# Making the next group's weights behind the up product instead of between the two products of a step

## The chip, the cores and the metric

The kernel runs on one core of one Trainium2 chip. The metric is the device time of one execution in microseconds. The engines are named as in the profile: PE is the matmul engine (PEld its weight loads), DVE the vector engine, ACT the activation engine, POOL and SP the two that mostly issue DMAs.

## What is computed

The reference is one inference step of a trunk layer with attention, retention and, last, an expert retrieval (PEER). Only the last part matters here. For every token, 128 of 16384 single-neuron experts are picked (8 heads, 16 each), and

```python
act = jax.nn.gelu(jnp.einsum('thkd,td->thk', u_table[eidx], xb), approximate=False)
return jnp.einsum('thk,thkd->td', g * act, v_table[eidx])
```

There are 1152 tokens, 1024 features, and tables `u_table` and `v_table` of 16384 x 1024.

## The kernel before

The stage that the change touches, `stage_experts`, treats the tokens in two ways. The first 384 tokens (three tiles of 128, "sparse") gather their experts' rows by indirect DMA (L2019); DVE multiplies them (L2107 in the first half, L2120 in the second). The other 768 tokens ("dense") go through all 16384 experts, in two groups of 384 tokens. A group takes J = 128 steps. Step n loads 128 experts' columns of u and v and does:

- the **down product** (`down`, L2193 to L2202): `p_a` = u times h, 24 matmuls of 384 columns, in three parts: u_hi with h_hi, u_hi with h_lo, u_lo with h_hi. `p_a` is one PSUM bank and not doubled, so the product waits until the GELU of the step before has read it (`gelu_full`). It also waits for `u_hi` (ACT, L1976) and, before its last 8 matmuls, for `u_lo` (DVE, L2082).
- the GELU (ACT, L1986), which reads `p_a`, and DVE's product of it with the experts' weights of these tokens (L2095), split into `g_hi` (L2098) and `g_lo` (L2100).
- the **up product** (`up`, L2204 to L2233): `p_y` += g times v, 18 matmuls of 512 columns, which need `g_hi`, `v_lo` and `g_lo`.

The weights of a group are a dense table that has to be made first: WeightSteps makes it in 96 steps of 4 tokens. DVE makes one-hot tiles `hot_j`, `hot_i` and `hot_w` (L1791 to L1795), PE multiplies them with 8 matmuls of 128 columns into the bank `pw` (`tensor`, L1804), and ACT copies `pw` out to `wt` (`scalar`, L1812, called the **copy** below). The first group's weights are made ahead of the loop. The second group's are made inside the first group's loop, one weight step in each of its first 96 turns. There is one bank `pw` there (`one_bank`).

`blocks` (L1885) writes the loop of every engine. One turn j calls `pre` for step j + 2 and `post` for step j + 1. On PE `pre` is the down product and `post` the up product, and the weight step of turn j stands between them. On ACT, whose `late` is set, a turn is `u_hi` of step j + 2, the GELU of step j + 1, `v_hi` of step j + 2 and then the copy of weight step j:

```python
                pre(j + (o + 2), j + 2, s)
                if weighted and not late:
                    weights(j + w.STEPS, s)
                post(j + (o + 1), j + 1, 1 - s)
```

On DVE a turn is `u_lo` of step j + 2, the one-hot tiles of weight step j, the three small products of step j + 1, the sparse products of one rank, and `v_lo` of step j + 2. Every engine runs its queue in the order written; engines are tied to each other by semaphores alone. The copy waits for `pw_full`, which PE's last matmul of the weight step raises.

Of the kernel before, what the change touches and what calls it, by code (L numbers as in the profile page):

```python
# [1080 lines left out]
def wait_count(eng, sem, count):  # L1081

    if not isinstance(count, int) or count > 0:
        eng.wait_ge(sem, count)
# [737 lines left out]
def stage_experts(nc, sem, m, keep, a):  # L1822
# [16 lines left out]
    w = WeightSteps(nc, sem, m, keep, keep.pairsT[:, 2, DENSE_AT:DENSE_AT + N_KEYS * WeightSteps.IN // 2].bitcast(F16))  # L1839
# [13 lines left out]
    one_bank = [pw[:]]  # L1853
# [24 lines left out]
    def weight_steps(eng, body):  # L1878
        body(0, 0)
        body(1, 1)  # L1880
        with eng.Fori(1, w.STEPS // 2) as k:
            for s in range(2):
                body(k * 2 + s, s)

    def blocks(eng, g, pre, post, first=lambda: None, between=lambda: None, weights=lambda n, s: None, late=None, rest=lambda n: None, unroll=False):  # L1885

        both = lambda n, j, s: (pre(n, j, s), late(n, j, s) if late else None)  # L1890
        o = g * J
        both(o, 0, 0)
        both(o + 1, 1, 1)
        first()
        post(o, 0, 0)
        between()

        def turn(k, weighted):
            for s in range(2):
                j = k * 2 + s  # L1900
                pre(j + (o + 2), j + 2, s)
                if weighted and not late:
                    weights(j + w.STEPS, s)
                post(j + (o + 1), j + 1, 1 - s)
                if late:
                    late(j + (o + 2), j + 2, s)
                if weighted and late:
                    weights(j + w.STEPS, s)
                rest(j)

        def turns(lo, hi, weighted):
            if unroll:
                for k in range(lo, hi):
                    turn(k, weighted)
            else:
                with eng.Fori(lo, hi) as k:
                    turn(k, weighted)

        done = w.STEPS // 2 if g < GROUPS - 1 else 0
        if done:  # L1920
            turns(0, done, True)
        turns(done, J // 2 - 1, False)
        post(o + J - 1, J - 1, 1)
# [5 lines left out]
    with nc.Block() as block:  # L1929

        @block.sync
        def _(sp):
            for s in range(SPARSE):
                sp.dma_start(hs[s], keep.h2_dram[:, :, s * P:(s + 1) * P]).then_inc(cols_in[s], 16)

            def load(n, j, s):
                wait_count(sp, ulo_full, n - 1)
                sp.dma_start(u_raw[s][:], a["uT"][j]).then_inc(u_in[s], 16)
                wait_count(sp, vlo_full, n - 1)
                sp.dma_start(v_raw[s][:], a["v"][j]).then_inc(v_in[s], 16)  # L1940

            for g in range(GROUPS):
                def first():
                    if g == 0:
                        w.store(sp, 0, w.stored)
                        with sp.Fori(1, BLOCKS) as b:
                            w.store(sp, b, w.stored)

                blocks(sp, g, load, lambda n, j, s: None, first)
            sp.wait_ge(ulo_full, GROUPS * J)  # L1950
            sp.wait_ge(vlo_full, GROUPS * J)
            for s in range(SPARSE):
                sp.dma_start(x1_sparse[s], keep.x1_dram[s]).then_inc(xs_in, 16)
            for s in range(SPARSE):
                sp.wait_ge(sparse_full, s + 1)
                sp.dma_start(out_rows(s), x1_sparse[s]).then_inc(sparse_out, 16)
            for i in range(GROUP):
                sp.wait_ge(y_full, (GROUPS - 1) * GROUP + i + 1)
                sp.dma_start(out_rows(SPARSE + (GROUPS - 1) * GROUP + i), x1[i][:]).then_inc(y_out[1][i], 16)
            sp.wait_ge(sparse_out, 16 * SPARSE)  # L1960
            for g in range(GROUPS):
                for i in range(GROUP):
                    sp.wait_ge(y_out[g][i], 16)
# [209 lines left out]
        @block.tensor  # L2173
        def _(pe):
            pe.sem_inc(w.pw_full, w.LEAD)
            pe.sem_inc(y_step, 1)
            for r in range(3):
                for s in range(SPARSE):
                    last = nc.tensor.transpose(p_idx[r][:, s * P:(s + 1) * P], keep.pairsT[:, r, s * P:(s + 1) * P], keep.ident)
            last.then_inc(idx_full, 1)  # L2180
            for s in range(SPARSE):
                pe.wait_ge(cols_in[s], 16)
                wait_count(pe, cols_read, s)
                for k in range(KD):
                    last = nc.tensor.transpose(p_h[:, k * P:(k + 1) * P], hs[s][:, k, :], keep.ident)
                last.then_inc(cols_turned, 1)
            weight_steps(pe, lambda n, s: w.tensor(pe, n, s, two_banks))
            pe.wait_ge(idx_done, 2)
            pe.wait_ge(cols_read, SPARSE)
            pe.wait_ge(w.pw_read, w.STEPS + w.LEAD)  # L2190

            for g in range(GROUPS):
                def down(n, j, s):  # L2193
                    pe.wait_ge(uhi_full, n + 1)
                    wait_count(pe, gelu_full, n)
                    for k in range(KD):
                        nc.tensor.matmul(p_a[:, 0:GT], u_hi[s][:, k, :], h_hi[:, k, :], start=k == 0, stop=False)  # L2197
                        nc.tensor.matmul(p_a[:, 0:GT], u_hi[s][:, k, :], h_lo[:, k, :], start=False, stop=False)  # L2198
                    pe.wait_ge(ulo_full, n + 1)
                    for k in range(KD):  # L2200
                        last = nc.tensor.matmul(p_a[:, 0:GT], u_lo[s][:, k, :], h_hi[:, k, :], start=False, stop=k == KD - 1)  # L2201
                    last.then_inc(a_full, 1)  # L2202

                def up(n, j, s):  # L2204
                    pe.wait_ge(ghi_full, n + 1)
                    pe.wait_ge(vlo_full, n + 1)
                    first, end = (isinstance(j, int) and j == x for x in (0, J - 1))
                    if first:
                        wait_count(pe, y_mul, g * GROUP)

                    def product(i, part, vv, begin, stop):
                        for half in range(2):
                            last = nc.tensor.matmul(p_y[i][:, half, :], part[s][:, i * P:(i + 1) * P], vv[s][:, half * 512:(half + 1) * 512],  # L2213
                                                    start=begin, stop=stop)
                        return last

                    if end:
                        pe.wait_ge(glo_full, n + 1)
                        for i in range(GROUP):
                            product(i, g_hi, v_hi, False, False)  # L2220
                            product(i, g_hi, v_lo, False, False)
                            last = product(i, g_lo, v_hi, False, True)
                            last.then_inc(y_tile, 1)
                        pe.wait_ge(y_tile, (g + 1) * GROUP)
                        pe.sem_inc(y_step, 1)
                        return
                    for i in range(GROUP):
                        product(i, g_hi, v_hi, first, False)
                        product(i, g_hi, v_lo, False, False)
                    pe.wait_ge(glo_full, n + 1)  # L2230
                    for i in range(GROUP):
                        last = product(i, g_lo, v_hi, False, False)
                    last.then_inc(y_step, 1)  # L2233

                pe.wait_ge(h_lo_full, g + 1)
                blocks(pe, g, down, up, weights=lambda n, s: w.tensor(pe, n, s, one_bank))

# [120 lines left out]
```

## Time and profile before

| | us |
|---|---|
| median of 3 runs | 4092.27 (4087.77 to 4099.85) |
| the profiled execution | 4092.37 |
| its span (first to last instruction) | 4090.6 |
| outside the span | 1.8 |

The execution is profiled once. In the views a row of the timeline is: start in us, duration in us, engine, line and operation, out<-in, and in brackets the idle time of that engine before it with what ended it. Matmuls are pipelined: a record's duration contains a tail that overlaps the next matmul, so the pace of PE is read from starts and not from durations. The first group's loop with weight steps runs from about 1882 to 2755 us, the second group's loop from about 2800 to 4050 us.

### The profile page before, as it was taken

How to read it: one execution, taken by the hardware profiler on the slowest of the kernel's cores; microseconds unless marked ns; L12 is line 12 of the kernel's file. 1: busy time of each engine (PE TensorE's matmuls, PEld its weight loads, DVE VectorE, ACT ScalarE, POOL GpSimd, SP SyncE). 2: the span in 40 equal slices, each digit the busy share in tenths (PEclk: the TensorE clock that was granted, in tenths of full speed). 3: DMA queues.
4: the chain of work that ended last, by engine and by line, in shares of the span. 5: the costliest groups of instructions: out<-in, count | busy, mean ns of one | idle time of the engine just before them, and what ended most of it. 6: DMA issues, size and time to landing. Idle time of an engine off the chain costs nothing.

```text
span 4090.6 us, 58626 instructions
## 1 busy us (share of the span) xinstructions
PE 3728.8 (91%) x19218; PEld 3036.7 (74%) x19218; DVE 2990.6 (73%) x5999; ACT 1231.1 (30%) x1750; POOL 1675.8 (41%) x1065
## 2 busy tenths in 40 slices
PE   8799988997669997278999999999999999999998
PEld 1699964665554443157888888888988999999997
DVE  0322273333534999798999999998889888888888
ACT  0411052222222222273333333332332233223222
POOL 0222100000311232204555555555557677777764
PEclk9799987998789999558999999999999999999999
DMA  7288713665241010348999999999999999999997
GB/s 255 100 267 288 253 38 103 205 201 188 80 150 52 31 36 21 113 185 289 331 339 343 349 340 342 343 339 363 341 307 370 361 340 340 344 335 344 331 347 256
DMA packets 302338, 1018.08 MB, mean 249 GB/s; under 512 B 30410, under 2 KB 61932, under 8 KB 294948
## 3 DMA queue, kind: packets, MB, share of 16 engines
q1 hardware_dynamic: 153348, 483.34, 35.1%
q0 software_dynamic: 128880, 486.07, 32.5%
q10 hardware_dynamic: 20016, 47.66, 3.0%
q8 instruction: 30, 0.49, 0.1%
q14 instruction: 64, 0.52, 0.0%
HBM read 875.22 MB, written 141.72 MB: 249 GB/s over the span
## 4 chain that ended last, share of the span: by engine, by line
PE 31%; DVE 14%; DMA 6%; issue 6%; POOL 1%; ACT 0%; DVEq 0%; ACTq 0%; SPq 0%; POOLq 0%
PE p_y L2213 16%; DVE rows L2107 6%; PE p_a L2201 5%; PE p_a L2198 5%; PE p_a L2197 5%; DMA rows<-u_rows,pairsT 5%; DVE u_lo L2082 2%; DVE v_lo L2089 2%; DVE hot_w L1795 1%; POOL rows L2019 1%; DVE pairsT L2095 1%; DVE g_hi L2098 1%; DMA rows<-in_v,pairsT 1%; DVE hot_j L1791 1%; DMA w_ring<-weights_spill 0%
## 5 line engine op out<-in xcount | busy, mean ns | idle before, releaser
L2019 POOL DMA_INDIRECT rows<-in_v,pairsT x384 | 730.2, 1902 | 300.5 <-DVE h_rows L2120 207.5
L2019 POOL DMA_INDIRECT rows<-u_rows,pairsT x384 | 594.8, 1549 | 492.2 <-DVE pairsT L2107 419.8
L2197 PE MATMUL p_a<-h_hi,u_hi 128*128 128x384 f32 x2048 | 687.5, 336 | 4.1 <-DVE h_lo L2160 2.4
L2198 PE MATMUL p_a<-h_lo,u_hi 128*128 128x384 f32 x2048 | 691.0, 337 | 0.0
L1981 ACT ACTIVATE v_hi<-v_raw 128x1024 fp32r<-128x1024 f32 x256 | 272.0, 1063 | 750.1 <-PE p_y L2213 735.5
L2213 PE MATMUL p_y<-v_hi,g_hi 128*128 128x512 f32 x1536 | 489.7, 400 | 7.9 <-DVE g_hi L2098 7.5
L2107 DVE CUSTOM_DVE_ANT_0 rows<-rows,h_rows 128x1024 f32<-128x1024 f32 x384 | 451.6, 1221 | 53.8 <-DMA rows<-u_rows,pairsT 51.1
L2120 DVE SCALAR_TENSOR_TENSOR h_rows<-rows,pairsT,h_rows 128x1024 f32<-128x1024 f32 x381 | 467.8, 1280 | 18.9 <-DMA rows<-in_v,pairsT 18.9
L2213 PE MATMUL p_y<-v_lo,g_hi 128*128 128x512 f32 x1536 | 478.6, 393 | 0.0
L2201 PE MATMUL p_a<-h_hi,u_lo 128*128 128x384 f32 x2048 | 400.1, 336 | 20.6 <-DVE u_lo L2082 20.6
L2197 PEld LDWEIGHTS p_a<-h_hi,u_hi 128*128 128x128 f32 x2048 | 385.3, 188 | 15.1 <-issue 4.6
L2198 PEld LDWEIGHTS p_a<-h_lo,u_hi 128*128 128x128 f32 x2048 | 385.1, 188 | 9.8
L2213 PE MATMUL p_y<-v_hi,g_lo 128*128 128x512 f32 x1536 | 390.6, 389 | 0.0
L2201 PEld LDWEIGHTS p_a<-h_hi,u_lo 128*128 128x128 f32 x2048 | 359.3, 188 | 25.1 <-DVE u_lo L2082 25.1
L2213 PEld LDWEIGHTS p_y<-v_lo,g_hi 128*128 128x128 f32 x1536 | 289.9, 189 | 66.4
L2213 PEld LDWEIGHTS p_y<-v_hi,g_lo 128*128 128x128 f32 x1536 | 288.7, 188 | 60.0
L2213 PEld LDWEIGHTS p_y<-v_hi,g_hi 128*128 128x128 f32 x1536 | 280.2, 189 | 54.6 <-DVE g_hi L2098 10.2
L2082 DVE TENSOR_TENSOR u_lo<-u_raw,u_hi 128x1024 fp32r<-128x1024 f32 x256 | 311.9, 1219 | 6.0 <-ACT u_hi L1976 6.0
L2089 DVE TENSOR_TENSOR v_lo<-v_raw,v_hi 128x1024 fp32r<-128x1024 f32 x256 | 312.4, 1221 | 1.3 <-issue 1.0
L1812 ACT ACTIVATE wt<-pw 128x512 f32 (+1 forms) x144 | 156.3, 1085 | 409.8 <-PE pw L1804 399.1
L1976 ACT ACTIVATE u_hi<-u_raw 128x1024 fp32r<-128x1024 f32 x256 | 270.0, 1055 | 4.8 <-DMA u_raw<-in_uT 4.8
L1522 PE MATMUL psc<-wc,hs 128*128 128x512 f32 x576 | 251.5, 595 | 0.0
(308 smaller groups left out, 5625.9 us busy)
## 6 DMA issues: line engine op xcount, KB each, us to landing
u_raw<-in_uT SPq DMA_DIRECT2D x256, 512.0 KB
v_raw<-in_v SPq DMA_DIRECT2D x256, 512.0 KB
w_ring<-weights_spill POOLq DMA_DIRECT2D x32, 1536.0 KB
u_rows<-pairsT ACTq DMA_DIRECT2D x64, 512.0 KB
key_cols<-in_uT SPq DMA_DIRECT2D x64, 512.0 KB, 4.1
u_rows<-key_rows SPq DMA_DIRECT2D x64, 512.0 KB
wada<-in_w_ada SPq DMA_DIRECT2D x12, 2048.0 KB, 8.0
weights_spill<-wt SPq DMA_DIRECT2D x24, 1024.0 KB, 3.9
```

What stands on the lines that cost most here:

```text
L1522: last = nc.tensor.matmul(psc[:, 4 * b:4 * b + 4, :], hs[:, k, :], wc[:, k, 4 * b:4 * b + 4, :], start=k == 0, stop=k == KD - 1)
L1976: nc.scalar.activation(u_hi[s][:], u_raw[s][:], ACT.Copy).then_inc(uhi_full, 1)
L1981: nc.scalar.activation(v_hi[s][:], v_raw[s][:], ACT.Copy).then_inc(vhi_full, 1)
L2019: pool.indirect_dma_start(rows[s][n % SLOTS][:], None, (keep.u_rows, v_rows)[g], at).then_inc(rows_in[s][n % SLOTS], 16)
L2082: nc.vector.tensor_sub(u_lo[s][:], u_raw[s][:], u_hi[s][:].bitcast(F32)).then_inc(ulo_full, 1)
L2089: nc.vector.tensor_sub(v_lo[s][:], v_raw[s][:], v_hi[s][:].bitcast(F32)).then_inc(vlo_full, 1)
L2107: nc.vector.tensor_tensor_reduce(out=slot[:], in0=slot[:], in1=keep.h_rows[:, s, :], op0=ALU.mult, op1=ALU.add, scale=1.0, scalar=0.0, acc ...
L2120: nc.vector.scalar_tensor_tensor(out=total, in0=slot[:], scalar=share, in1=total, op0=ALU.mult, op1=ALU.add).then_inc(rows_used, 1)
L2197: nc.tensor.matmul(p_a[:, 0:GT], u_hi[s][:, k, :], h_hi[:, k, :], start=k == 0, stop=False)
L2198: nc.tensor.matmul(p_a[:, 0:GT], u_hi[s][:, k, :], h_lo[:, k, :], start=False, stop=False)
L2201: last = nc.tensor.matmul(p_a[:, 0:GT], u_lo[s][:, k, :], h_hi[:, k, :], start=False, stop=k == KD - 1)
L2213: last = nc.tensor.matmul(p_y[i][:, half, :], part[s][:, i * P:(i + 1) * P], vv[s][:, half * 512:(half + 1) * 512], start=begin, stop=stop)
```

## The change

`blocks` gets a parameter `after`. PE alone passes `after=True`, and with it the weight step of a turn stands behind `post` (the up product) instead of between `pre` and `post`. The other engines' code is the same.

```diff
-    def blocks(eng, g, pre, post, first=lambda: None, between=lambda: None, weights=lambda n, s: None, late=None, rest=lambda n: None, unroll=False):
+    def blocks(eng, g, pre, post, first=lambda: None, between=lambda: None, weights=lambda n, s: None, late=None, rest=lambda n: None, unroll=False, after=False):
...
                 pre(j + (o + 2), j + 2, s)
-                if weighted and not late:
+                if weighted and not late and not after:
                     weights(j + w.STEPS, s)
                 post(j + (o + 1), j + 1, 1 - s)
+                if weighted and after:
+                    weights(j + w.STEPS, s)
                 if late:
                     late(j + (o + 2), j + 2, s)
...
-                blocks(pe, g, down, up, weights=lambda n, s: w.tensor(pe, n, s, one_bank))
+                blocks(pe, g, down, up, weights=lambda n, s: w.tensor(pe, n, s, one_bank), after=True)
```

The first place on PE is the seam between the down and the up product of a turn in the first group's loop. Lines behind L1902 are numbered two higher in the changed kernel. `p_a<-h_hi,u_lo` is the end of the down product, `pw` the weight step, `p_y` the up product. Before:

```order
L2201 MATMUL p_a<-h_hi,u_lo 128x384 x8
L1800 REGISTER_ALU
L1801 REGISTER_ALU
L1804 MATMUL pw<-hot_w,hot_i 128x128 x8
L2213 MATMUL p_y<-v_hi,g_hi 128x512 x2
```

In the changed kernel:

```order
L2200 MATMUL p_a<-h_lo,u_hi 128x384
L2203 MATMUL p_a<-h_hi,u_lo 128x384 x8
L2215 MATMUL p_y<-v_hi,g_hi 128x512 x2
L2215 MATMUL p_y<-v_lo,g_hi 128x512 x2
L2215 MATMUL p_y<-v_hi,g_hi 128x512 x2
```

The eight matmuls into `pw` and the two register instructions ahead of them have left this place.

The second place on PE is the seam between the up product of one turn and the down product of the next. Before:

```order
L2213 MATMUL p_y<-v_lo,g_hi 128x512 x2
L2213 MATMUL p_y<-v_hi,g_lo 128x512 x6
L2194 REGISTER_ALU
L2197 MATMUL p_a<-h_hi,u_hi 128x384
L2198 MATMUL p_a<-h_lo,u_hi 128x384
```

In the changed kernel:

```order
L2215 MATMUL p_y<-v_hi,g_lo 128x512 x6
L1800 REGISTER_ALU
L1801 REGISTER_ALU
L1804 MATMUL pw<-hot_w,hot_i 128x128 x8
L2196 REGISTER_ALU
L2199 MATMUL p_a<-h_hi,u_hi 128x384
L2200 MATMUL p_a<-h_lo,u_hi 128x384
```

The weight step is now the last thing ahead of the next down product.

ACT's queue keeps its order. This is one turn's copy (`wt<-pw`) and what follows it in the changed kernel (`pairsT<-p_a` is the GELU):

```order
L1812 ACTIVATE wt<-pw 128x4x128
L1978 ACTIVATE u_hi<-u_raw 128x1024
L1986 REGISTER_ALU
L1988 ACTIVATE pairsT<-p_a 128x384
L1983 ACTIVATE v_hi<-v_raw 128x1024
```

Nothing moved here: `u_hi` of the next turn and the GELU stand behind the copy, before and now.

## Rows read from the trace of the kernel before

**Rows 1.** The page: granted clock in 40 slices; the chain by engine

```profile
PEclk9799987998789999558999999999999999999999
...
PE 31%; DVE 14%; DMA 6%; issue 6%; POOL 1%; ACT 0%; DVEq 0%; ACTq 0%; SPq 0%; POOLq 0%
```

**Rows 2.** Busy time by stretch: window, length, engines, clock, DMA share, GB/s

```profile
2000.00:2700.00 700.00, 693.11 (x3901) 619.46 (x3900) 660.54 (x1167) 264.72 (x312) 389.58 (x263) 1.00 0.95 342
3000.00:4000.00 1000.00, 996.11 (x5034) 905.87 (x5033) 893.34 (x970) 301.51 (x361) 709.15 (x381) 1.00 0.96 343
```

**Rows 3.** Waits from 1880 to 2750 us: total us, times, longest us

```profile
ACT wt L1812 <- PE pw L1804: 379.4, 94, 10.6
...
PE p_a L2201 <- DVE u_lo L2082: 15.0, 10, 4.8
```

**Rows 4.** Timeline of one turn, first group's loop with weight steps

```profile
2007.78 0.64 PE L1804 MATMUL pw<-hot_w,hot_i 128*128 128x128 f16 x8
...
2008.23 0.71 PE L2213 MATMUL p_y<-v_hi,g_hi 128*128 128x512 f32 x2
...
2008.77 1.11 ACT L1812 ACTIVATE wt<-pw 128x512 f32 x1 [3.86 <-PE pw L1804]
...
2009.67 1.08 ACT L1976 ACTIVATE u_hi<-u_raw 128x1024 fp32r<-128x1024 f32 x1
...
2010.63 0.48 ACT L1986 ACTIVATE pairsT<-p_a 128x384 f32<-128x384 f32 x1
2010.78 1.23 DVE L2082 TENSOR_TENSOR u_lo<-u_raw,u_hi 128x1024 fp32r<-128x1024 f32 x1 [0.25 <-ACT u_hi L1976]
...
2012.20 0.19 PEld L2197 LDWEIGHTS p_a<-h_hi,u_hi 128*128 128x128 f32 x1
...
2013.85 0.36 DVE L2098 CAST g_hi<-pairsT 128x384 fp32r<-128x384 f32 x1
...
2015.22 1.55 PE L2201 MATMUL p_a<-h_hi,u_lo 128*128 128x384 f32 x8
...
2016.62 0.64 PE L1804 MATMUL pw<-hot_w,hot_i 128*128 128x128 f16 x8
...
2017.06 0.70 PE L2213 MATMUL p_y<-v_hi,g_hi 128*128 128x512 f32 x2
...
2017.60 1.10 ACT L1812 ACTIVATE wt<-pw 128x512 f32 x1 [3.85 <-PE pw L1804]
```

**Rows 5.** Timeline of PE alone: five idle times between 2.6 and 3.2 us

```profile
2780.14 2.16 PE L2201 MATMUL p_a<-h_hi,u_lo 128*128 128x384 f32 x8 [2.68 <-DVE u_lo L2082]
...
1963.31 1.66 PE L2201 MATMUL p_a<-h_hi,u_lo 128*128 128x384 f32 x8 [2.69 <-DVE u_lo L2082]
...
1588.05 1.09 PE L1516 MATMUL pT<-grid,xn 128*128 128x128 f32 x8 [2.71 <-ACT xn L1587]
...
1192.27 1.91 PE L1548 MATMUL psc<-sc 128*128 128x128 f32 x15 [2.83 <-ACT wc L1619]
...
1039.03 0.63 PE L1207 MATMUL bank_qf<-grid,qf 128*128 128x128 f32 x4 [3.17 <-issue]
```

**Rows 6.** Busy time in short stretches behind these idle times, columns as Rows 2

```profile
2778.00:2782.00 4.00, 1.86 (x8) 1.86 (x9) 3.93 (x6) 0.00 (x0) 2.60 (x2) 0.89 0.88 284
2782.00:2786.00 4.00, 4.00 (x14) 3.24 (x14) 4.00 (x7) 0.49 (x1) 2.61 (x2) 0.69 0.96 370
...
1963.00:1967.00 4.00, 3.50 (x22) 2.95 (x23) 3.11 (x8) 1.21 (x2) 2.10 (x2) 1.00 1.02 329
...
1589.00:1593.00 4.00, 0.49 (x4) 0.38 (x3) 4.00 (x4) 3.55 (x9) 2.27 (x1) 0.61 0.00 0
...
1193.00:1197.00 4.00, 3.15 (x28) 2.96 (x26) 1.38 (x2) 1.19 (x2) 0.00 (x0) 1.00 0.41 136
...
1039.00:1043.00 4.00, 3.97 (x25) 4.00 (x25) 1.38 (x2) 1.88 (x2) 2.42 (x2) 0.66 0.00 0
```

**Rows 7.** Busy time while the first group's weights are made, columns as Rows 2

```profile
1750.00:1800.00 50.00, 36.82 (x286) 27.32 (x284) 49.44 (x144) 37.63 (x37) 0.00 (x0) 0.50 0.46 189
```

## The prediction

> **What bounds the kernel now.** I read the page's slices first, then busy time by stretch, then the waits of the stretch that the change touches, then the timeline of one turn. The clock line shows where the two dense groups run: the last twenty slices or so, almost all at full clock [rows 1]. By stretch, PE is busy for 693 of 700 us in the first group's loop and 996 of 1000 us in the second, where no weights are made [rows 2]. Both are at granted clock 1.00, that is 2.4 GHz. DVE follows at 661 of 700 us. The chain of waits names PE most [rows 1]. So in the first group's loop PE sets the pace and DVE has little to spare. ACT is busy for 265 of 700 us, and the waits say what it does with the rest: for 379 us, in 94 waits, it stood in front of the copy of `pw` until PE had made it [rows 3].
>
> The timeline of a turn shows the pace: the weight step starts at 2007.78 and again at 2016.62, so a turn lasts 8.84 us [rows 4]. Within it PE does the weight step (2007.78 to 2008.23, 0.45 us), the up product until about 2012.4, and the down product until the next weight step. The reader should see one thing more. ACT's copy starts at 2008.77, 0.99 us behind the start of the weight step; `u_hi` of the next turn starts at 2009.67, the GELU at 2010.63, and it ends at 2011.11. ACT had been idle for 3.86 us before the copy, though `u_raw` and `p_a` were there earlier: these two stand behind the copy in its queue and are held up by it. PE needs both of their results for the next down product, whose first weight load starts at 2012.20. They were ready 1.09 us before that. The up product, some 4 us of PE's own work, is what hides the copy, `u_hi` and the GELU.
>
> **What the change removes and adds.** No instruction comes or goes. PE still does 8 matmuls into `pw` in each of 96 turns, 0.45 us of its time, and the two register instructions move along. Removed is the weight step from the seam between down and up product: the up product can start 0.45 us earlier behind the down product. This is worth nothing by itself, since PE is full. Nor does it uncover a wait: `g_hi` starts at 2013.85 and takes 0.36 us, so it is there at 2014.21, and the up product starts at 2017.06 [rows 4], 2.85 us later; 0.45 us less leaves 2.4.
>
> Added is a closed chain at the other seam. PE's weight step ends the turn; ACT's copy waits for it; `u_hi` and the GELU stand behind the copy; and PE's next down product waits for both. The up product that used to cover this now stands ahead of it. Nothing else lies between, so PE stands still. Step by step from the start of the weight step [rows 4]: 0.99 us to the start of the copy, 0.90 to the start of `u_hi`, 0.96 to the start of the GELU, 0.48 for the GELU: 3.33 us. PE has worked 0.45 of this. Its restart is not seen in these rows; the starts behind other waits bound it between 0 and some 0.3 us (the weight load of 0.19 us at 2012.20 and a hand-over), and I take 0.17. The stall is 3.33 - 0.45 + 0.17 = 3.05 us in each turn, between 2.9 and 3.2. In the profile it will read about 0.2 less, since a record of matmuls has a tail (0.64 us for the weight step, against 0.45 to the next start [rows 4]).
>
> Who else waits? DVE's `u_lo` waits for `u_hi` (0.25 us now [rows 4]) and comes later by the same amount; the down product needs `u_lo` only for its last 8 matmuls, some 2.8 us behind its start, and `u_lo`, which starts with the GELU and takes 1.23 us against its 0.48, ends some 0.7 us behind the start. DVE is behind `u_lo` as it was, and a turn of nearly 12 us is longer than its 8.4 us of work (661 us in 79 turns [rows 2]), so it will be idle instead of late. `v_hi` stands behind the GELU and is not needed before the up product of a later step. POOL's and SP's queues are tied to DVE's and PE's progress and get slack. The next turn's one-hot tiles are made long before PE asks for them, and the bank `pw` is free, since the copy is in the chain anyway. So the chain closes on PE alone: 8.84 + 3.05 = 11.89 us for a turn at full clock, and 96 x 3.05 = 293 us in all.
>
> **The clock.** A stall of this size in every turn can also lower PE's clock. The trace has five idle times of PE between 2.6 and 3.2 us [rows 5]. Behind the one of 2.68 us the clock was 0.89 and 0.69 in the two next stretches of 4 us [rows 6]: at the lower of the two levels, 1.2 GHz, that is 2 x (0.11 + 0.31) x 4 = 3.4 us. Behind the one of 2.69 us it stayed at 1.00, behind 2.71 it fell (0.61), behind 2.83 it stayed, behind 3.17 it fell (0.66) [rows 5, 6]. So three of five fell, and length alone did not decide. My stall reads as 2.85 us, in the upper part of these. A fall costs half of the low stretch, since PE has nothing but work then: 1.7 us. Per turn the price lies between 0 and 1.7 us. I take nine falls in ten, 1.5 us, nearer the upper end: the stall is longer than four of the five, and where three of five idle times single out at random fall, a stall in every turn meets any condition that depends on when it comes.
>
> The Trainium skill, "TensorE: Matmul & The Clock Gate", section "HAM oscillation — how this bites in real kernels", says that a loop in which PE waits between bursts of matmuls can start every pass at the lower clock. By that rule the price is the full 1.7 us, and the sum below would be 4540 us; the two idle times without a fall (2.69 and 2.83 us [rows 5, 6]) do not follow it.
>
> **The sum.** 8.84 + 3.05 + 1.5 = 13.4 us for a turn. 96 x 4.55 = 437 us. Against this, PE's present waits for `u_lo` in this loop, 15.0 us in 10 waits [rows 3], come from gathers that are late for DVE; with several us to spare in each turn about half of them should vanish: -8 us. Against the profiled execution's 4092.4 us, which is the median of the runs within 0.1 us, this gives 4092 + 437 - 8 = 4521 us.
>
> **Rivals.**
>
> *The clock stays up.* Then only the stall is paid: 4092 + 293 - 8 = 4377 us, or 4363 to 4391 for stalls of 2.9 to 3.2 us. For it speak the idle times of 2.69 and 2.83 us; against it the other three, and that there are 96 stalls to come.
>
> *The clock stays down for longer.* If a low stretch lasts twice as long (it was 3.4 us in the clean case, but PE at half speed meets its next stall sooner), the price is 3.4 us: 96 x 6.45 - 8 = 611, so 4703 us. While the first group's weights are made, the clock stood at 0.50 throughout with PE busy for 36.8 of 50 us [rows 7]. Those are short bursts, with a pause about every 1.4 us; here PE works for over 8 us without a break, so this is the lesser case.
>
> *The other side: the copy is not what holds ACT up.* If ACT could take `u_hi` and the GELU ahead of the copy, or if PE's down product did not have to wait for the GELU, the chain would be open. The up product would start 0.45 us earlier, PE would remain full, and the time would be 4092 us, or some 15 us less if the 0.16 us of pause in front of the weight step vanished with its move (96 x 0.16). It decides from where the GELU would end less than 0.45 us behind the weight step's start. The queue's order and the single bank `p_a` speak against it: the GELU started at 2010.63, 2.85 us behind the start of the weight step, and its input stands ahead of that step on PE, so it waited for nothing but the queue.
>
> *The change does less than it says*, because some turns are not reached by it: the new order stands in the one loop body that runs all 96 turns, so there is little room.
>
> **How the numbers follow.** The forecast, a closed chain with a fall of the clock in most turns: 0.70. Clock stays up: 0.13. Clock down for longer: 0.11. Something between the forecast and the second: 0.03. Not slower: 0.03. The forecast's own bounds are 96 x (2.9 + 1.0) to 96 x (3.2 + 1.8), which is 4459 to 4564 us. The range is to leave out no more than 2 in 10: it takes in the case with full clock, 4363, and ends at 4600, a little above the forecast's own upper bound, since that bound knows the low stretch from one clean case; it leaves out most of the last two cases. A measurement of this kernel can tell 0.3% from no change, some 12 us. Faster by over 0.3%: 0.01. Within 0.3%: 0.02. Slower: 0.97.
>
> **What would show it.** The waits should have a row that isn't there now, PE's first down matmul waiting for ACT's GELU, about 96 times for 2.85 us, some 275 us in total. The starts of the weight steps should be 13.4 us apart, or 11.9 where the clock is up. The distances on ACT from copy to `u_hi` to GELU should be the same 0.9 and 0.96 us. The granted clock in this loop should be near 0.88 (low for about 3.1 of 13.4 us), DVE's share should fall from 94% to some 62%, and the second group's loop should be as before. The forecast is wrong if PE's wait is for something else, if it is under 2.5 us, or if the clock is 1.00 throughout.

## The result

The changed kernel took 4467.01 us (median of 4 runs, 4464.08 to 4469.12) against 4090.02 us for the kernel before in the same comparison (4083.7 to 4099.85). The ratio of the times is 1.0919, with a 95% interval of 1.0895 to 1.0942. It is slower by 377 us; 4521 us was predicted, with a range of 4363 to 4600.

The page of the changed kernel, sections 2 and 4 (the chain of waits by engine, then by line), answers to [rows 1]:

```profile
PEclk9899889996899975688888889889999999999999
...
PE 50%; issue 5%; ACT 3%; DVE 1%; ACTq 1%; DMA 1%; POOL 0%; SPq 0%; DVEq 0%; POOLq 0%
PE p_y L2215 23%; PE p_a L2199 9%; PE p_a L2200 9%; PE p_a L2203 8%; ACT u_hi L1978 2%; PE pw L1804 1%; ACT pairsT L1988 1%; DMA rows<-in_v,pairsT 1%; ACTq L1812 1%; DVE h_rows L2122 0%; POOL rows L2021 0%; DMA w_ring<-weights_spill 0%; ACTq L1809 0%; ACTq L1918 0%; DVE u_lo L2084 0%
```

Two things are new. In the first group's loop the clock line now has eights, where the kernel before has nines, and ACT is in the chain: its lines for `u_hi` and for the GELU (`pairsT`), and L1812 on ACT's own sequencer (ACTq), which is register work for the copy.

Busy time by stretch in the changed kernel (window, length, PE, PEld, DVE, ACT, POOL, clock, DMA share, GB/s), for the two groups' loops, answers to [rows 2]:

```profile
2000.00:3100.00 1100.00, 873.18 (x4236) 780.77 (x4235) 722.54 (x1270) 268.62 (x336) 411.26 (x286) 0.89 0.71 237
3400.00:4400.00 1000.00, 997.49 (x5035) 907.65 (x5034) 890.21 (x969) 299.79 (x360) 728.57 (x386) 1.00 0.96 343
```

The second group's loop is what it was: 5035 matmuls in 1000 us against 5034. In the first group's loop PE is busy for 79% where it was 99%, DVE for 66% where it was 94%, and the clock is 0.89.

The matmuls of the weight steps in this loop, by line, in the kernel before (first row) and in the changed one (second row), with the starts of the first and the last matmul:

```profile
L1804 PE MATMUL pw<-hot_w,hot_i x768: 218/218/330, 1881.9 to 2745.4; 128*128 128x128 f16 x192
```

```profile
L1804 PE MATMUL pw<-hot_w,hot_i x768: 218/218/234, 1889.8 to 3125.4; 128*128 128x128 f16 x192
```

They are 96 steps of 8. The mean turn was 863.5 / 95 = 9.09 us and is 1235.6 / 95 = 13.01 us. (The last matmul starts 0.4 us behind the start of its step; this adds under 0.005 us to either mean.) That is 372 us in 95 turns, of 376.7 us by which the spans differ (4467.3 against 4090.6). So the loss lies in this loop.

The waits of the changed kernel from 1880 to 3130 us (who waited for whom: us in total, times, longest us) answer to [rows 3]:

```profile
ACT wt L1812 <- PE pw L1804: 939.3, 96, 10.2
...
DVE u_lo L2084 <- ACT u_hi L1978: 419.1, 96, 8.0
PE p_a L2199 <- ACT pairsT L1988: 259.3, 96, 2.8
```

The row that the prediction asked for is there: PE's first down matmul waits for ACT's GELU, 96 times, 2.70 us each. PE's wait for `u_lo` [rows 3] is gone from this stretch.

The timeline of one seam in the changed kernel answers to [rows 4]:

```profile
2410.74 0.64 PE L1804 MATMUL pw<-hot_w,hot_i 128*128 128x128 f16 x8
2411.72 1.02 ACT L1812 ACTIVATE wt<-pw 128x512 f32 x1 [10.06 <-PE pw L1804]
2412.55 1.05 ACT L1978 ACTIVATE u_hi<-u_raw 128x1024 fp32r<-128x1024 f32 x1
2413.49 0.48 ACT L1988 ACTIVATE pairsT<-p_a 128x384 f32<-128x384 f32 x1
...
2414.12 0.41 PE L2199 MATMUL p_a<-h_hi,u_hi 128*128 128x384 f32 x1 [2.75 <-ACT pairsT L1988]
```

Read from top to bottom it is the closed chain: weight step, copy 0.98 us later, `u_hi` 0.83 us later, GELU 0.94 us later, 0.48 us for it, and PE 0.15 us behind its end. From the weight step's start to the next down product are 3.38 us; the weight step's own work is 0.45 of them.

The starts of three weight steps in a row in the timeline of PE alone, with the restarts between them, show two kinds of turns:

```profile
2372.43 0.64 PE L1804 MATMUL pw<-hot_w,hot_i 128*128 128x128 f16 x8
2375.72 0.45 PE L2199 MATMUL p_a<-h_hi,u_hi 128*128 128x384 f32 x1 [2.66 <-ACT pairsT L1988]
2384.14 0.64 PE L1804 MATMUL pw<-hot_w,hot_i 128*128 128x128 f16 x8
2387.53 0.46 PE L2199 MATMUL p_a<-h_hi,u_hi 128*128 128x384 f32 x1 [2.74 <-ACT pairsT L1988]
2397.48 0.64 PE L1804 MATMUL pw<-hot_w,hot_i 128*128 128x128 f16 x8
```

From 2372.43 to 2384.14 are 11.71 us, from 2384.14 to 2397.48 are 13.34. Over the 95 distances 18 are short (mean 11.72) and 77 long (mean 13.30). The idle time is 2.69 us on the mean of the short ones and 2.70 on that of the long ones; what differs is how long PE's work behind it takes. (The restarts come 3.29 and 3.39 us behind the weight step in turn, here as in the whole loop, so the mean is 3.34.) Busy time in stretches of 4 us in the changed kernel, columns as before, shows why:

```profile
2398.00:2402.00 4.00, 1.35 (x7) 1.24 (x6) 1.63 (x3) 3.20 (x4) 2.06 (x2) 0.93 0.99 375
2402.00:2406.00 4.00, 4.00 (x17) 4.00 (x17) 3.93 (x9) 0.00 (x0) 0.19 (x1) 0.65 0.97 322
2406.00:2410.00 4.00, 4.00 (x20) 3.41 (x19) 2.97 (x5) 0.00 (x0) 3.51 (x2) 1.00 0.97 296
```

Behind the idle time that ends at 2400.77 the clock stood at its lower level of 1.2 GHz for 2 x (0.07 + 0.35) x 4 = 3.4 us, with PE busy all the while.

### The profile page after: what moved, and what is told of

It is laid out like the page before. It is cut to its first block, busy times and chain, and to the rows that moved or that the text cites. A ratio compares the mean times of both kernels' runs of the same rounds, so it can differ in the third digit from the quotient of the medians.

```text
span 4467.3 us, 58626 instructions
## 1 busy us (share of the span) xinstructions
PE 3866.1 (87%) x19218; PEld 3162.8 (71%) x19218; DVE 2989.5 (67%) x5999; ACT 1211.8 (27%) x1750; POOL 1667.8 (37%) x1065
## 4 chain that ended last, share of the span: by engine, by line
PE 50%; issue 5%; ACT 3%; DVE 1%; ACTq 1%; DMA 1%; POOL 0%; SPq 0%; DVEq 0%; POOLq 0%
PE p_y L2215 23%; PE p_a L2199 9%; PE p_a L2200 9%; PE p_a L2203 8%; ACT u_hi L1978 2%; PE pw L1804 1%; ACT pairsT L1988 1%; DMA rows<-in_v,pairsT 1%; ACTq L1812 1%; DVE h_rows L2122 0%; POOL rows L2021 0%; DMA w_ring<-weights_spill 0%; ACTq L1809 0%; ACTq L1918 0%; DVE u_lo L2084 0%
## 5 line engine op out<-in xcount | busy, mean ns | idle before, releaser
L2199 PE MATMUL p_a<-h_hi,u_hi 128*128 128x384 f32 x2048 | 770.7, 376 | 263.4 <-ACT pairsT L1988 260.6
L2021 POOL DMA_INDIRECT rows<-u_rows,pairsT x384 | 578.5, 1506 | 830.4 <-DVE pairsT L2109 752.1
L2200 PE MATMUL p_a<-h_lo,u_hi 128*128 128x384 f32 x2048 | 765.3, 374 | 0.0
L2199 PEld LDWEIGHTS p_a<-h_hi,u_hi 128*128 128x128 f32 x2048 | 438.1, 214 | 286.2 <-ACT u_hi L1978 138.9
L2200 PEld LDWEIGHTS p_a<-h_lo,u_hi 128*128 128x128 f32 x2048 | 441.4, 216 | 6.1
L1812 ACT ACTIVATE wt<-pw 128x512 f32 (+1 forms) x144 | 148.9, 1034 | 958.9 <-PE pw L1804 958.9
L2203 PEld LDWEIGHTS p_a<-h_hi,u_lo 128*128 128x128 f32 x2048 | 370.5, 193 | 2.8 <-DVE u_lo L2084 2.8
```

Of the source, the lines that this page charges most:

```text
L2021: pool.indirect_dma_start(rows[s][n % SLOTS][:], None, (keep.u_rows, v_rows)[g], at).then_inc(rows_in[s][n % SLOTS], 16)
```

## The experiments

Theory A is that of the prediction: PE's weight step, ACT's copy, `u_hi`, the GELU and PE's next down product form a closed chain, because the copy stands ahead of the other two in ACT's queue, and a second term is the lower clock behind each stall. Theory B is that the weight step's new place costs by itself, by its own waits or the single bank. Theory C is that the low clock and not the stall does most of the harm. The late copy, with either order on PE, the covered chain and the 14 matmuls of zero weights ran together; the kernel before took 4092.82 us among them. The expectations count 78 turns with a fall of the clock where the distances show 77.

### Opening the chain in ACT's queue

```diff
                 post(j + (o + 1), j + 1, 1 - s)
...
+                if behind and weighted and not (isinstance(j, int) and j == 0):
+                    weights(j + (w.STEPS - 1), 1 - s)
...
-                if weighted and late:
+                if weighted and late and not behind:
                     weights(j + w.STEPS, s)
...
-                blocks(act, g, split, gelu, first, between, weights=lambda n, s: w.scalar(act, n, s, one_bank), late=split_v)
+                blocks(act, g, split, gelu, first, between, weights=lambda n, s: w.scalar(act, n, s, one_bank), late=split_v, behind=True)
```

> The changed kernel with one thing more: in ACT's queue the copy of a weight step stands one turn later, behind the GELU of the next turn, so that `u_hi` and the GELU no longer stand behind it. PE's order is that of the changed kernel. Theory A (closed chain PE weight step, ACT copy, `u_hi`, GELU, PE down product): the stall goes, turns are 8.8 us again, granted clock 1.00 in the loop, and the time is 4065 to 4095 us. Theory B (the weight step's new place costs by itself, by its waits or by the single bank `pw`): nothing changes, some 4467 us, turns of 13.0 us. Theory C (the stall is real but short, and the low clock does most of the harm): as A, so this run tells A and C from B only.

It took 4089.08 us, 0.9989 of the kernel before (0.9980 to 0.9999). The timeline of the weight steps and of ACT in it:

```profile
2396.03 0.64 PE L1804 MATMUL pw<-hot_w,hot_i 128*128 128x128 f16 x8
2397.01 1.09 ACT L1812 ACTIVATE wt<-pw 128x512 f32 x1 [4.42 <-PE pw L1804]
2397.88 1.08 ACT L1992 ACTIVATE v_hi<-v_raw 128x1024 fp32r<-128x1024 f32 x1
2398.84 1.06 ACT L1987 ACTIVATE u_hi<-u_raw 128x1024 fp32r<-128x1024 f32 x1
2400.94 0.49 ACT L1997 ACTIVATE pairsT<-p_a 128x384 f32<-128x384 f32 x1 [1.04 <-PE p_a L2212]
2404.86 0.64 PE L1804 MATMUL pw<-hot_w,hot_i 128*128 128x128 f16 x8
```

Turns are 8.84 us, in 83 of 95, with the weight step where the change put it. Late turns are still there: the mean of all is 9.11, against 9.09 in the kernel before. The copy still waits for PE (4.42 us), but `u_hi` and the GELU are no longer behind that wait: the GELU now follows the end of its own input (`p_a`). This throws out theory B. The new place costs nothing by itself; all 377 us hang on what stands behind the copy in ACT's queue.

### Covering part of the chain

The weight step stands inside the up product, ahead of its last six matmuls.

```diff
...
                     for i in range(GROUP):
                         product(i, g_hi, v_hi, first, False)
                         product(i, g_hi, v_lo, False, False)
+                    inside()
                     pe.wait_ge(glo_full, n + 1)
...
```

> The changed kernel, but the weight step stands inside the up product, ahead of its last six matmuls (the `g_lo` part, 1.35 us of PE's work), so these six cover part of ACT's chain. Theory A: the stall is 2.87 - 1.35 = 1.5 us, turns are 10.35 us, PE's wait for the GELU reads about 1.35 us, the clock stays at 1.00, and the time is 4090 - 23 + 96 x 1.52 = 4213 us. If idle times of this size lower the clock as often as those of the changed kernel do, 4340 us. Theory B (any place but the old one costs the same): 4467 us.

It took 4216.70 us, 1.0301 (1.0284 to 1.0318). The waits from 1880 to 2880 us and the timeline of PE in it:

```profile
PE p_a L2200 <- ACT pairsT L1989: 123.4, 96, 1.4
```

```profile
2396.77 0.64 PE L1804 MATMUL pw<-hot_w,hot_i 128*128 128x128 f16 x8
...
2407.13 0.64 PE L1804 MATMUL pw<-hot_w,hot_i 128*128 128x128 f16 x8
```

This turn is 10.36 us, the mean of all 10.42, and PE's wait 1.29 us. The distance from weight step to restart is unchanged, and each microsecond of PE's own work that is put into it is a microsecond less of stall. The clock was 1.00 from 2000 to 2800 us.

### Filling the stall with work that adds nothing

```diff
...
+                def filled(n, s):
+                    w.tensor(pe, n, s, one_bank)
+                    for x in range(FILL):
+                        nc.tensor.matmul(p_y[0][:, 0, 0:N_KEYS * w.IN], zeros[:], w.iota.rearrange("p k b -> p (k b)"), start=False, stop=False)
...
-                blocks(pe, g, down, up, weights=lambda n, s: w.tensor(pe, n, s, one_bank), after=True)
+                blocks(pe, g, down, up, weights=filled, after=True)
```

> The changed kernel with more work: behind each weight step in the loop PE does 14 matmuls of 256 columns with zero weights into `p_y` (0.107 us each, 1.5 us in all), which add nothing to the result. They lie in the stall. Theory A with the clock as a second term: the stall stays 2.87 us from the weight step on, but PE is idle for only some 1.2 us of it, the clock no longer falls, all turns are 11.7 us, and the time is 4467 - 78 x 1.59 = 4343 us. If the clock has no part in it: 4467 us. If PE were not waiting there at all, the filling is added: 4467 + 96 x 1.5 = 4611 us.

It took 4344.12 us, 1.0612 (1.0594 to 1.0630): 123 us less than the changed kernel, with 1344 matmuls more. The timeline of PE and busy time in its loop:

```profile
2406.09 1.69 PE L2247 MATMUL p_y<-pairsT,zeros 128*128 128x256 f16 x14
2409.01 0.41 PE L2205 MATMUL p_a<-h_hi,u_hi 128*128 128x384 f32 x1 [1.24 <-ACT pairsT L1991]
```

```profile
2000.00:2800.00 800.00, 719.21 (x4361) 628.70 (x4360) 581.06 (x1024) 218.81 (x272) 334.90 (x229) 1.00 0.77 263
```

The clock is 1.00, all 95 turns are between 11.70 and 11.83 us, and the distance from weight step to restart is 3.40 us as it was. So the loss parts into two: the stall, less the late turns of the kernel before that it swallows, is worth 4344 - 4093 = 251 us, and the clock 4467 - 4344 = 123 us. (The 4467 come from another comparison; by the ratios, 1.0919 - 1.0612, it is 126 us, and by the turns, 77 x 1.58, it is 122.) Theory C falls: a third of the loss is the clock's.

### Fewer zeros

The same with `FILL = 5`.

> As e4_fill, with 5 matmuls of zero weights instead of 14, 0.53 us, so that PE's idle time reads about 2.15 us: between the 1.24 us at which the clock never fell and the 2.70 us at which it fell in four turns of five. Turns without a fall are 11.7 us in any case. The time says how often it falls: 4343 us for never, 4467 us for as often as in the changed kernel. By a price that grows with the length of the idle time, some 4400 us.

It took 4462.73 us, 1.0910 (1.0891 to 1.0928). It ran together with the next two kernels; the kernel before took 4090.12 us among them. Its waits from 1880 to 3130 us:

```profile
PE p_a L2205 <- ACT pairsT L1991: 206.9, 96, 2.2
```

PE is idle for 2.16 us a turn instead of 2.70, and nothing is won that can be told from none: 77 of 95 turns are long (13.30 us), as many as in the changed kernel. The price of the clock doesn't grow with the idle time between these two; the guess of some 4400 us was wrong.

### A shorter and a longer copy

In the first the copy in this loop takes one token's part of `pw`, so three quarters of the second group's weights are left out of the computation. In the second ACT copies `pw` once more beforehand, to a tile that nobody reads.

```diff
...
+        o, i = out.rearrange("p j b -> p b j"), banks[s % len(banks)]
+        if len(banks) == 1:
+            o, i = o[:, 0:1, :], i[:, 0:1, :]
+        self.nc.scalar.activation(o, i, ACT.Copy, scale=1.0 / SHARE_UNIT).then_inc(self.pw_read, 1)
```

> The changed kernel, but in the first group's loop ACT's copy takes a quarter of `pw` (one token's 128 columns of 512), so three quarters of the second group's weights are left out. Theory A: the distance from the start of the copy to `u_hi` falls from 0.83 us to some 0.3, the stall from 2.87 to some 2.35 us, and turns without a fall of the clock from 11.7 to 11.2 us. If the clock falls as often as in the changed kernel (78 of 95 turns, 1.59 us each), 4467 - 96 x 0.53 = 4416 us; if it falls in half of the turns, 4367 us; if never, 4292 us. Theory B (the copy is not in the chain, PE waits for something else behind the weight step): 4467 us.

```diff
     def scalar(self, act, n, s, banks):
+        if len(banks) == 1:
+            act.wait_ge(self.twice, n - (self.STEPS - 1))
+            act.wait_ge(self.pw_full, n + (self.LEAD + 1))
+            self.nc.scalar.activation(self.scratch[:], banks[0], ACT.Copy, scale=1.0 / SHARE_UNIT).then_inc(self.twice, 1)
```

> The changed kernel, with ACT copying `pw` twice in the loop, the first time to a tile that nobody reads. Theory A: the chain is longer by one copy, 0.85 us, so the stall is 3.7 us and a turn without a fall 12.6 us: 4467 + 96 x 0.85 = 4549 us, and up to 4577 us if the clock now falls in every turn. If the low clock is what sets the loop and the idle time only its cause, the time hardly moves from 4467 us.

The quarter copy took 4376.06 us, 1.0700 (1.0682 to 1.0718). ACT's timeline in it:

```profile
2406.48 0.38 ACT L1815 ACTIVATE wt<-pw 128x128 f32 x1 [10.11 <-PE pw L1804]
2406.94 1.06 ACT L1981 ACTIVATE u_hi<-u_raw 128x1024 fp32r<-128x1024 f32 x1
...
2417.81 0.39 ACT L1815 ACTIVATE wt<-pw 128x128 f32 x1 [8.48 <-PE pw L1804]
2418.00 1.05 ACT L1981 ACTIVATE u_hi<-u_raw 128x1024 fp32r<-128x1024 f32 x1
```

`u_hi` follows at 0.46 and 0.19 us in turn instead of 0.83, and the shortest turn is 11.11 us instead of 11.69 (the mean of the short ones is 11.19 against 11.72). The copy's length is in the chain. Only 50 of 95 turns are long. The expectation had 4416 us for as many long turns as in the changed kernel, and 27 fewer at 1.58 us each make that 4373, 3 us from what was measured. Its idle time (211.3 us in 96 waits, 2.20 each on the mean) is that of the five zeros' kernel within 0.04 us, which had 77.

The double copy took 4498.25 us, 1.0997 (1.0979 to 1.1016), less than the 4549 us expected. Its timeline:

```profile
2406.45 0.64 PE L1806 MATMUL pw<-hot_w,hot_i 128*128 128x128 f16 x8
2407.12 0.60 ACT L1814 ACTIVATE weights_scratch<-pw 128x512 f32<-128x512 f32 x1 [9.80 <-PE pw L1806]
2407.62 1.02 ACT L1818 ACTIVATE wt<-pw 128x512 f32 x1
2408.45 1.05 ACT L1985 ACTIVATE u_hi<-u_raw 128x1024 fp32r<-128x1024 f32 x1
```

The expectation was off in two things. The added copy is not a second 0.85 us: it writes a contiguous tile and takes 0.50 us to the next start, where the real one, which writes with a stride, takes 0.83. And it starts 0.67 us behind the weight step, where the real copy starts 0.98 behind it. Most of the other 0.31 us is to be seen in the rows of the copy's line in the changed kernel (count, then ns, then first and last start), two on ACT's own sequencer and the copy:

```profile
L1812 ACTq FUSED_REGOPS  x92: 203/203/203, 1903.7 to 3087.3; - x92
L1812 ACTq ALU_OP  x92: 35/35/35, 1903.9 to 3087.5; - x92
L1812 ACT ACTIVATE wt<-pw x92: 1023/1024/1048, 1904.0 to 3087.6; 128x512 f32 x92
```

They are register work for the real copy's address, 0.24 us. It starts some 0.7 us behind the start of the weight step (the first row at 1903.7, its weight step at 1903.0), so behind the wait, and ends ahead of the copy. The run with the late copy has the same copy without it, in a turn written out singly, with a fixed address:

```profile
1884.28 0.64 PE L1804 MATMUL pw<-hot_w,hot_i 128*128 128x128 f16 x8
1885.02 1.11 ACT L1812 ACTIVATE wt<-pw 128x512 f32<-128x512 f32 x1 [4.17 <-PE pw L1804]
```

There it starts 0.74 us behind the weight step. So 0.25 us of the 0.31 are the register work; where the other 0.06 come from is not shown. In the run with two copies the register work runs beside the added copy. This row also shows that the fixed address is not what makes the added copy short: with the stride it takes 1.11 us. So the chain is 0.50 - 0.31 = 0.19 us longer; long turns are 13.49 us against 13.30, and 86 of them instead of 77. 95 x 0.19 + 9 x 1.58 = 32 us, and 31 were measured over the changed kernel.

### Looking for a better kernel

The late copy with the old order on PE, then the same again in more rounds, and with the weight step inside the down product, ahead of the matmuls that wait for `u_lo`. The edits are those shown above, the last one with `inside()` in `down`.

> The kernel before, with the copy one turn later in ACT's queue as in e1_copy_late; PE's order is that of before. Theory A: PE stays full in this loop and sets 8.83 us a turn; `u_hi` comes earlier, DVE no longer waits for it, and the turns that gathers made late (mean turn 9.09 us in the kernel before) get shorter by up to 0.25 us on average: 4066 to 4090 us. Rival: DVE's late gathers set those turns alone and nothing changes, 4090 us within 5.

> The same kernel as e2_copy_late_old_order, measured in more rounds, since its ratio there (0.9988, 0.9979 to 0.9998) is near what can be told from no change: 4088 us against 4092, or no difference at all.

> e2_copy_late_old_order, with the weight step one place earlier on PE: inside the down product, ahead of its last eight matmuls, which are the ones that wait for DVE's `u_lo`. Where gathers make `u_lo` late (nine or ten turns of 96, 1 to 3 us each in e2), 0.45 us of PE's work now covers part of it. By this, up to 10 x 0.45 = 4 us less than e2: 4082 to 4088 us. If the late turns are bound by DVE for longer than PE's slack, nothing changes: 4088 us. The copy has even more time ahead of it, so no stall as in the changed kernel.

The first took 4087.83 us, 0.9988 (0.9979 to 0.9998). The other two ran together, the kernel before at 4088.28 us among them: the same again took 4082.92 us, 0.9985 (0.9976 to 0.9994), and the one with the weight step inside the down product 4087.05 us, 0.9995 (0.9986 to 1.0004). The late copy wins 0.1%, a little beyond what its interval leaves open, and nothing to build on. The matmuls of the weight steps by line, in the repeated run:

```profile
L1804 PE MATMUL pw<-hot_w,hot_i x768: 218/218/330, 1879.3 to 2734.1; 128*128 128x128 f16 x192
```

The mean turn is 854.8 / 95 = 9.00 us against 9.09: the late turns shrank a little, the others stayed at PE's 8.84. The place inside the down product brings nothing that can be told from none over the kernel before, and over the late copy alone, which it was to better by up to 4 us, it is 4 us slower.

## Why the prediction was right, and where its sizes were off

**What bounds.** Right. PE's own work of 8.84 us sets the turn as long as ACT's chain is hidden: opening the chain gives 8.84 us with either order on PE.

**The chain and who waits.** Right in mechanism and in each link. The wait named is there 96 times. No other engine came to the bound: DVE was idle for 419 us waiting for `u_hi`, and the up product did not wait for anything. The other signs came too: turns of 13.30 and 11.72 us (13.4 and 11.9 were said), a granted clock of 0.89 (0.88), DVE at 66% (62%). That `u_hi` and the GELU are held up by the queue and by nothing else is shown by the run with the late copy; before it was read from the rows alone.

**The stall, 3.05 us.** It was 11.72 - 8.84 = 2.88 us, 0.17 less, which is 16 us in 96 turns. The links add up to 0.98 + 0.83 + 0.94 + 0.48 + 0.15 = 3.38 us in the seam shown, of which the weight step covers 0.45. The restart, guessed at 0.17 us, is 0.15 in one turn and 0.05 in the next, 0.10 on the mean; with it the links give 3.33 - 0.45 = 2.88. The largest other miss is the copy, 0.83 us to the next start where [rows 4] have 0.90; it takes 1.02 us in the stall, 1.10 in the kernel before and in the run with the late copy. That PE is idle while ACT copies is not the reason: in the runs with the covered chain and with the filled stall PE works all through the copy, which takes 1.03 and 1.04 us. The rows of these two (all copies of the first, min/median/max in ns, and one of the second):

```profile
L1812 ACT ACTIVATE wt<-pw x96: 1027/1031/1102, 1885.5 to 2875.0; 128x512 f32 x96
```

```profile
2406.59 1.04 ACT L1812 ACTIVATE wt<-pw 128x512 f32 x1 [8.49 <-PE pw L1804]
```

What goes with the longer copy is DVE at work. In the kernel before DVE works during nearly every copy, in the changed kernel during almost none; and in the run with the covered chain the four copies during which it works throughout take 1.09 us, the other 92 1.03. No run was made for it alone, so this stays a reading.

**The clock, 1.5 us a turn.** There are six idle times of this length in the kernel before, and not five; the sixth (2.92 us, at 149 us) tells nothing, since the clock was low ahead of it too. The kind was right and the size a little high: a fall costs 13.30 - 11.72 = 1.58 us, not 1.7, and comes in 77 of 95 turns (0.81), not in nine of ten. That is 1.28 us a turn; the miss is 21 us. The low stretch was 3.4 us, as in [rows 6]. The rule of the Trainium skill ("TensorE: Matmul & The Clock Gate", "HAM oscillation — how this bites in real kernels") is that a loop in which PE waits between bursts can start every pass at the lower clock; the waits in its example are longer than those here. In this kernel the clock falls in four turns in five, and in none where the idle time is 1.2 to 1.3 us. The prediction said that the length of the idle time alone does not decide. The runs bear that out: 2.16 us gave 77 falls, 2.20 us gave 50, 2.70 us gave 77 and 2.88 us, with two copies, gave 86. What does decide beside the length is not shown; the runs with 2.16 and 2.20 us also differ in the length of a turn at full clock, 11.7 and 11.2 us. So nine in ten was a guess that came near, and not a rule that was tested.

**The waits that vanish, 8 us.** Under-sized, and the step that failed most clearly. The prediction took half of PE's 15 us of idle time in front of `u_lo` [rows 3]. But the late turns cost the kernel before more than that row has: its mean turn was 9.09 us, and 95 x (9.09 - 8.84) = 24 us. (Some 3 us of these are the clock's, which was low for 6.8 us behind the idle time of 4.8 us in this loop:

```profile
1974.00:1978.00 4.00, 0.42 (x1) 0.42 (x2) 3.99 (x8) 0.00 (x0) 3.42 (x2) 0.70 0.96 336
1978.00:1982.00 4.00, 4.00 (x18) 3.60 (x18) 3.93 (x9) 0.26 (x1) 0.59 (x2) 0.50 1.01 351
1982.00:1986.00 4.00, 4.00 (x18) 3.26 (x18) 4.00 (x7) 2.08 (x3) 3.41 (x2) 0.95 0.76 253
```

The last column but two is the granted clock.) In the changed kernel the whole of it is gone, since no turn stands out. The mean turn should have been taken from the first and the last weight step, and not 8.84 us from one undisturbed turn.

**The sum.** 16 + 21 + 16 = 53 us are the three misses, all to the same side; predicted and measured are 4521 and 4467, 54 us apart. Of the 54 us 2 are the base's, since the kernel before was at 4090 in this comparison and not at 4092; the three misses are good to a few us.

**The rivals.** "The clock stays up" said 4377 us; the kernel with the filled stall is that case and took 4344, again lower by the stall's and the late turns' misses. "The clock stays down for longer" did not come. "Not slower" fell with the queue's order, and the run with the late copy shows that it would have been right had ACT not had the copy in front. The 15 us that this rival thought possible on top did not come: that run is 4 us below the kernel before.

## What to carry to other kernels

When a producer's step is moved behind work that used to follow it, look not at who reads its result but at what stands behind the reader in the reader's queue. The price is the length of that stretch of queue plus hand-overs, less the work that still covers it, and it can be read from one turn's timeline. Take the mean turn from many turns, and count a second price for the clock if PE will be idle in every turn for long enough; here 2.2 us and more had that price and 1.3 us had none.

## What was not expected of the hardware

- More work made the kernel faster: 14 matmuls with zero weights in each stall, 1344 in all, took 123 us off, because the granted clock stayed at 1.00 instead of 0.89. Five matmuls in each took off nothing that can be told from none (4463 us).
- Of the 0.98 us from the weight step to ACT's copy, 0.25 us is register work for an address, done only when the wait in front of it is over. With a fixed address the copy started 0.74 us behind the weight step.
- ACT's copy of 512 columns took 0.60 us to a contiguous tile and 1.02 us to a strided one, in the same turn.
